# A sparse expert FFN on one core: experts dealt one by one to the shorter of two sequences, in place of two fixed lists

## What is computed

```python
logits = h @ router_w + router_b
top_v, top_i = lax.top_k(logits, 4)
top_w = softmax(top_v)
# for each expert e, over the tokens sent to it:
z = h[tok] @ w1[e] + b1[e]                 # w1[e]: 1024 x 2048
z_glu, z_lin = split(z, 2)
z_glu = min(z_glu, 7); z_lin = clip(z_lin, -7, 7)
act = z_glu * sigmoid(1.702 * z_glu) * (z_lin + 1)
y = act @ w2[e] + b2[e]                    # w2[e]: 1024 x 1024
# h + g2 * (sum of the token's four y * weight), then a final RMSNorm
```

## Time and profile before

| what | value |
|---|---|
| median of 3 runs | 1625.52 us |
| profiled execution, its own time | 1622.66 us |
| its span | 1620.8 us |
| PE busy / DVE / ACT / POOL | 91% / 45% / 16% / 13% of the span |
| weights and other data over the DMA queues | 497.13 MB, mean 307 GB/s |
| chain that ended last | PE 64%, DMA 20%, SP's queue 9%, DVE 4% |
| FFN loop, first to last step end (L1392) | 541.2 to 1583.3 us |

### The profile page before, as it was taken

The page is one execution under the profiler, slowest core; times in us unless marked ns, Lnnn a source line. Parts: engine busy times, 40 slices in busy tenths (PEclk is TensorE's granted clock), DMA queues, the critical chain, the costliest instruction groups (busy, mean ns, idle before and its releaser), DMA issues.

```text
span 1620.8 us, 39662 instructions
## 1 busy us (share of the span) xinstructions
PE 1478.6 (91%) x14640; PEld 739.7 (46%) x14640; DVE 734.9 (45%) x2468; ACT 251.7 (16%) x434; POOL 211.5 (13%) x263
## 2 busy tenths in 40 slices
PE   5999999999895988999799899999889979998897
PEld 3658888888552332333234234343233324343333
DVE  4403877777647432434244244434233424343344
ACT  4403555555322000000000000000000000000001
POOL 1000000000151111212121121212111211111120
PEclk9999999999997998999899899999799979999998
DMA  8685111112667898948989989999899989999878
GB/s 358 200 269 148 55 53 52 52 52 56 240 289 289 352 419 332 417 191 359 414 340 404 413 341 405 417 415 418 327 417 416 418 328 418 417 414 417 331 307 308
DMA packets 130869, 497.13 MB, mean 307 GB/s; under 512 B 15372, under 2 KB 48492, under 8 KB 94908
## 3 DMA queue, kind: packets, MB, share of 16 engines
q1 hardware_dynamic: 122588, 479.99, 75.2%
q0 software_dynamic: 8256, 16.81, 2.8%
HBM read 484.92 MB, written 17.58 MB: 310 GB/s over the span
## 4 chain that ended last, share of the span: by engine, by line
PE 64%; DMA 20%; SPq 9%; DVE 4%; issue 2%; ACT 1%; POOL 0%; DVEq 0%; POOLq 0%; ACTq 0%
PE ps L1777 24%; PE ps L1815 12%; DMA big_b<-in_moe_w 10%; DMA arena<-in_moe_w 8%; PE ps L1474 6%; SPq L435 6%; PE ps L1475 6%; PE ps L1476 6%; SPq L429 3%; PE ps L1653 3%; PE ps L1585 1%; PE ps L1497 1%; DMA ring_t<-in_mod_c 1%; PE ps L1599 1%; PE ps L1594 1%
## 5 line engine op out<-in xcount | busy, mean ns | idle before, releaser
L1777 PE MATMUL ps<-arena,rows 128*32 128x512 f32 x2736 | 329.7, 617 | 36.2 <-DMA arena<-in_moe_w 32.8
L1777 PE MATMUL ps<-big_b,rows 128*32 128x512 f32 x2688 | 315.8, 605 | 24.3 <-DMA big_b<-in_moe_w 23.6
L1777 PEld LDWEIGHTS ps<-arena,rows 128*32 128x32 f32 x2736 | 87.1, 112 | 231.8 <-issue 153.2
L860 ACT ACTIVATE rows<-ps 128x256 f32<-128x256 f32 x84 | 32.2, 384 | 1032.2 <-issue 636.5
L1777 PEld LDWEIGHTS ps<-big_b,rows 128*32 128x32 f32 x2688 | 85.5, 111 | 212.8 <-issue 152.7
L1815 PE MATMUL ps<-big_b,rows 128*32 128x256 f32 x2688 | 165.9, 397 | 14.9 <-DMA big_b<-in_moe_w 14.9
L1815 PE MATMUL ps<-arena,rows 128*32 128x256 f32 x2688 | 166.1, 398 | 12.5 <-DMA arena<-in_moe_w 12.5
L1392 DVE SCALAR_TENSOR_TENSOR y_sb<-ps,w_s,g_q 128x256 f32<-128x256 f32 x42 | 20.3, 484 | 288.7 <-PE ps L1815 288.7
L1392 DVE SCALAR_TENSOR_TENSOR rows<-ps,w_s,g_q 128x256 f32<-128x256 f32 x42 | 20.3, 484 | 267.7 <-PE ps L1815 267.7
L1815 PEld LDWEIGHTS ps<-big_b,rows 128*32 128x32 f32 x2688 | 84.1, 114 | 77.2 <-DMA big_b<-in_moe_w 22.8
L1815 PEld LDWEIGHTS ps<-arena,rows 128*32 128x32 f32 x2688 | 84.6, 113 | 73.6 <-DMA arena<-in_moe_w 18.9
(11 more groups left out here) (361 smaller groups left out, 1768.7 us busy)
## 6 DMA issues: line engine op xcount, KB each, us to landing
big_b<-in_moe_w SPq DMA_DIRECT2D x192, 1024.0 KB, 15.4
arena<-in_moe_w SPq DMA_DIRECT2D x192, 1024.0 KB, 16.9
ring_t<-in_hg_w_in SPq DMA_DIRECT2D x32, 512.0 KB, 4.0
ogT<-in_mod_w SPq DMA_DIRECT2D x16, 1024.0 KB, 5.1
arena<-yrows SPq DMA_DIRECT2D x8, 1024.0 KB, 12.0
x_sb<-in_x SPq DMA_DIRECT2D x2, 2048.0 KB, 7.8
arena<-in_hg_w_in SPq DMA_DIRECT2D x4, 1024.0 KB, 25.6
arena<-in_mod_c SPq DMA_DIRECT2D x4, 1024.0 KB, 22.3
```

Source lines behind the costliest of these rows:

```text
L1777: last = mm(bank[q * G:(q + 1) * G, :], XT[par][:, pos * G:(pos + 1) * G], w[:, :, q * NW:(q + 1) * NW], start=(pos == 0), stop=False)
```

## The change

Both kernels deal the 32 experts to two sides. Before, which size rank goes to which side, and where in it, is fixed by two lists (STREAM). After, there is one list of ranks (ORDER); each expert in turn goes to the side that has fewer steps so far, behind those already there. If the two sides are equal the one that was dealt to last takes the next. The running totals are a prefix scan on DVE (`so_far`) and a recursion of 32 rounds on POOL with two `tensor_scalar` each (`ahead` is the longer side's total, `minus` its negative, a wait after each round). DVE makes of it each expert's side and first pair. The gather for step one moves into the middle of POOL's recursion. The matmuls of the table (formerly ahead of `slots_of(2)`) stand behind the fourth of the six early w1 chunks (TABLE_BEHIND = 3). On DVE much of the work that followed the table stands before it now, and `tab_ok` is raised after the one-hot of step two, not before it. Step one's one-hot has a buffer of its own (`pt1`), which frees `pt` for step two. Expert 1 also has at least one group. The table is shorter (NPAIR_MAX from 94 to 56).

```diff
-NPAIR_MAX = LAT * TOPK // G + E - 2
+NPAIR_MAX = (LAT * TOPK // G + E + LAT // G) // 2
-STREAM = ((0, 2, 5, 7, 6, 18, 16, 17, 23, 15, 31, 9, 26, 28, 21, 27),
-          (1, 19, 25, 29, 11, 24, 14, 22, 20, 13, 30, 12, 10, 8, 4, 3))
+ORDER = (0, 1, 11, 13, 10, 3, 29, 15, 22, 7, 18, 6, 31, 12, 8, 21, 2,
+         19, 27, 17, 28, 9, 20, 5, 23, 16, 4, 26, 24, 14, 25, 30)
+TABLE_BEHIND = 3
...
# POOL, behind the scatters
-            for par in range(2):
-                pool.wait_ge(S["idx_ok"], par + 1)
-                gather(par)
+            pool.wait_ge(S["idx_ok"], 1)
+            gather(0)
+            pool.wait_ge(S["row_ok"], 4)
+            for j in range(E):
+                if j == E // 2:
+                    pool.wait_ge(S["idx_ok"], 2)
+                    gather(1)
+                total = so_far[:, j + 1:j + 2]
+                me.mark(pool.tensor_scalar(ahead[:, j + 1:j + 2], minus[:, j:j + 1], total, ahead[:, j:j + 1],
+                                           ALU.add, ALU.max))
+                me.mark(pool.tensor_scalar(minus[:, j + 1:j + 2], ahead[:, j:j + 1], total, minus[:, j:j + 1],
+                                           ALU.subtract, ALU.min))
+                me.wait()
+            pool.sem_inc(S["dealt_ok"], 1)
...
# DVE, behind nr16
             dve.wait_ge(S["tab_ps"], 5)
-            me.mark(V.tensor_copy(tab_nn[:, :], ps[6][0:1, 100:102]))
...
+            V.tensor_tensor_scan(so_far[:, 1:E + 1], ones[0:E, 0:E], ps[6][0:E, 96:96 + E], 0.0, ALU.mult,
+                                 ALU.add).then_inc(S["row_ok"], 1)
+            hot_tile(2, slice(1, 2), pt1)
+            hot_tile(3, slice(1, 2), pt1)
+            choice(slice(1, 2), 1)
+            dve.wait_ge(S["xi_ps"], 2)
+            index(1, False)
+            next_slots()
+            transpose_x(0, 16)
...
+            dve.wait_ge(S["dealt_ok"], 1)
+            me.mark(V.tensor_tensor(more, ahead[:, 0:E], ahead[:, 1:E + 1], ALU.not_equal))
+            me.mark(V.tensor_tensor(dealt[:, 0, :], so_far[:, 0:E], ahead[:, 0:E], ALU.subtract))
+            me.wait()
+            me.link(V.tensor_tensor_scan(behind[:, 1:E + 1], more, none[:, :], 0.0, ALU.not_equal, ALU.add))
+            me.link(V.scalar_tensor_tensor(dealt[:, 1, :], behind[:, 0:E], float(4 * E), dealt[:, 0, :], ALU.mult, ALU.add))
+            me.link(V.tensor_tensor(dealt, dealt, ident[0:E, 0:E].unsqueeze(1).broadcast_to([E, 2, E]), ALU.mult))
+            me.link(V.tensor_reduce(at_2, dealt, AX_X, ALU.add))
+            me.mark(V.tensor_scalar(stb16, at_2[:, 0:1].broadcast_to([E, P]), float(G), None, ALU.mult))
+            me.mark(V.scalar_tensor_tensor(end_c, by_rank[:, 0:1], 1.0, at_2[:, 1:2], ALU.mult, ALU.add))
+            me.link(V.tensor_scalar(past[0:E], io_c[0:E], at_2[:, 1:2], None, ALU.is_ge))
             V.scalar_tensor_tensor(ind16, io_c[0:E], end_c, past[0:E], ALU.is_lt, ALU.mult).then_inc(S["row_ok"], 1)
...
             dve.wait_ge(S["tab_ps"], 6)
             me.link(V.tensor_scalar(bef[:, :], ps[7][:, 0:NBT], float(E), None, ALU.add))
             me.mark(V.tensor_copy(tab_e[:, :], bef[0:1, :]))
+            me.mark(V.scalar_tensor_tensor(dm, ranks, 1.0, msk, ALU.add, ALU.mult))
+            me.wait()
+            dve.sem_inc(S["y_ok"], 2)
+            one_hot(2, 0)
+            choose(0, 0)
             me.mark(V.tensor_scalar(tab_ld[:, :, 0], bef[0:1, :], float(E - 1), None, ALU.min))
...
             dve.sem_inc(S["tab_ok"], 1)
...
# PE, the early chunks of step 0
             for pos in range(AHEAD):
                 z_chunk(ps[2], 0, pos, 16)
+                if pos == TABLE_BEHIND:
+                    pe.wait_ge(S["row_ok"], 5)
+                    for i in range(LT):
+                        mm(ps[3][:, i * E:(i + 1) * E], stb16, rt16, start=False, stop=True, skip_group_check=True)
+                    mm(ps[7][:, 0:NBT], idb16, ind16, start=True, stop=True).then_inc(S["tab_ps"], 1)
             slots_of(3)
```

More of the change, by code:

```diff
@@ L186, in build @@
         nmax = rtake(LT)
-        pt0 = rtake(LT * P // 2).bitcast(BF16).rearrange("p (i s) -> p i s", i=LT)
+        pt0, pt1 = (rtake(LT * P // 2).bitcast(BF16).rearrange("p (i s) -> p i s", i=LT) for _ in range(2))
         es = rtake(LT)
-        cntc, nbc, start_c = (rtake(1) for _ in range(3))
+        cntc, nbc = (rtake(1) for _ in range(2))
         thr, over = rtake(LAT // G), rtake(LAT // G)
@@ L194, in build @@
         io_one = rtake(E)[0:E]
-        pick = rtake(2 * E)[0:E].rearrange("p (a e) -> p a e", a=2)
+        so_far, ahead, minus, behind = (rtake(E + 1)[0:E] for _ in range(4))
+        more = key
+        at_2 = rtake(2)[0:E]
+        pick = dealt = rtake(2 * E)[0:E].rearrange("p (a e) -> p a e", a=2)
         by_rank = rtake(2)[0:E]
@@ L199, in half @@
             return rtake(n // 2)[0:E].bitcast(BF16)
-        nb16, idb16, stb16 = half(P), half(P), half(P)
+        nb16, idb16 = half(P), half(P)
+        stb16 = nb16
         nr16, gt16, rt16 = half(E), half(E), half(E)
@@ L218, in build @@
         tab_ld = tab_words[:, 2:2 * NBT + 2].rearrange("p (b w) -> p b w", w=2)
-        tab_nf = rtake(NBT)[0:1]
+        tab_nf = past[0:1]
         tab_nn = sb("tab_nn", [1, 2])
@@ L226, in build @@
         seq = sb("seq", [E, E])
[L227 to L230, removed]
+        rank_c = sb("rank_c", [E, 1])
+        none = sb("none", [E, E])
         pmod = sb("pmod", [P, 1])
@@ L293, in build @@
         mod_used modq_ok bias_ok yo_ps h_ok stdev2_ok f_ok hT_ps hT_a hT_d lT_ps lT_ok lg_ps shb_ok cb_ps rw_ok
-        e_v_ok e_w_ok msk_ok tab_ps row_ok tab_ok
+        e_v_ok e_w_ok msk_ok tab_ps row_ok dealt_ok tab_ok
         frow_st frow_st1 pt_ok xi_ps idx_ok rows_ok go xt_ok z_ps sig_ok at_ok y_ok
@@ L553, in _ @@
             pool.tensor_copy(mk[:, :, :, :], mkf).then_inc(S["consts"], 1)
-            for side_n, order in enumerate(STREAM):
-                for n, rank in enumerate(order):
-                    me.mark(pool.memset(seq[:, rank:rank + 1], float(side_n * 2 * E + n)))
+            for n, rank in enumerate(ORDER):
+                me.mark(pool.memset(seq[:, n:n + 1], float(rank)))
+            me.mark(pool.memset(none[:, :], 0.0))
             me.wait()
@@ L594, in _ @@
                 me.mark(pool.memset(kb_row[:, n:n + 1], float((2 - n) * FAR)))
+            for t in (so_far, ahead, minus, behind):
+                me.mark(pool.memset(t[:, 0:1], 0.0))
             me.wait()
@@ L982, in _ @@
             me.link(V.tensor_tensor(ed_t, seq[:, :], ident[0:E, 0:E], ALU.mult))
[L983 to L990, removed]
+            me.link(V.tensor_reduce(rank_c[:, :], ed_t, AX_X, ALU.add))
             me.wait()
@@ L1287, in _ @@
             me.link(V.tensor_reduce(nbc[0:E], over[0:E], AX_X, ALU.add))
-            me.link(V.tensor_tensor(nbc[0:E], nbc[0:E], ident[0:E, 0:1], ALU.max))
+            me.link(V.scalar_tensor_tensor(nbc[0:E], kb_col, 0.0, nbc[0:E], ALU.is_gt, ALU.max))
             V.tensor_copy(nb16, nbc[0:E].broadcast_to([E, P])).then_inc(S["row_ok"], 1)
@@ L1310, in _ @@
             me.mark(V.tensor_copy(idb16, by_rank[:, 1:2].broadcast_to([E, P])))
-            hot_tile(1, slice(1, 2))
+            hot_tile(1, slice(1, 2), pt1)
             dve.wait_ge(S["tab_ps"], 5)
-            me.mark(V.tensor_copy(tab_nn[:, :], ps[6][0:1, 100:102]))
[L1315 to L1321, removed]
-            choice(slice(1, 2), 1)
[L1323 to L1337, removed]
+            V.tensor_tensor_scan(so_far[:, 1:E + 1], ones[0:E, 0:E], ps[6][0:E, 96:96 + E], 0.0, ALU.mult,
+                                 ALU.add).then_inc(S["row_ok"], 1)
+            hot_tile(2, slice(1, 2), pt1)
+            hot_tile(3, slice(1, 2), pt1)
+            choice(slice(1, 2), 1)
             dve.wait_ge(S["xi_ps"], 2)
             index(1, False)
+            next_slots()
             transpose_x(0, 16)
@@ L1351, in _ @@
             me.link(V.reciprocal(es, es))
-            me.link(V.tensor_tensor(wd, wd, es.unsqueeze(2).broadcast_to([P, LT, E]), ALU.mult))
[L1353 to L1356, removed]
+            dve.wait_ge(S["dealt_ok"], 1)
+            me.mark(V.tensor_tensor(more, ahead[:, 0:E], ahead[:, 1:E + 1], ALU.not_equal))
@@ new lines, in _ @@
+            me.mark(V.tensor_copy(tab_n[:, 0:1], ahead[0:1, E:E + 1]))
+            me.mark(V.tensor_copy(kw16[:, :, 1, 0:E], wd))
+            me.wait()
+            me.link(V.tensor_tensor(wd, wd, kw16[:, :, 1, 0:E], ALU.subtract))
+            me.link(V.tensor_copy(kw16[:, :, 2, 0:E], wd))
+            me.link(V.tensor_tensor(wd, wd, kw16[:, :, 2, 0:E], ALU.subtract))
+            me.mark(V.tensor_copy(kw16[:, :, 3, 0:E], wd))
+            me.wait()
+            me.mark(V.memset(tab_nf[:, 0:2], 0.0))
@@ L1357, in _ @@
+            dve.wait_ge(S["tab_ps"], 6)
+            me.link(V.tensor_scalar(bef[:, :], ps[7][:, 0:NBT], float(E), None, ALU.add))
+            me.mark(V.tensor_copy(tab_e[:, :], bef[0:1, :]))
```

(14 more changed lines are left out.)

10 lines of the change are left out of this document (5 added, 5 removed).

## The result

The changed kernel takes **1613.34 us** (median of 5 runs, 1612.45 to 1618.39). The ratio to the kernel before is 0.9932, with a 95% interval of 0.9915 to 0.9949 (five runs of the kernel before stood beside it, median again 1625.52). The forecast was 1596.5 with a range of 1585 to 1614; the median is just inside the range, but the gain is 12.2 us where 29.0 were foretold. The profiled execution took 1612.45 us, with a span of 1610.4.

A forecast was written before the change was run, and what follows sets the result against it. TensorE (10.87 us a step) and the weight queue (30.2 us an expert) limit the loop in turns. 1622.66 - 36.5 (waits) + 6 (table) + 1.5 (tail) = 1593.7 us profiled, 1596.5 against the median; range 1585 to 1614.

The forecast's parts named there:

- What bounds the loop, and the waits: Loop: TensorE and weight queue limit it in turns; closely spaced switches cause the waits, which fall from 140.1 by 36.5 us.
- The first switch's wait: Loop, first expert switch: a wait of 2.2 us, kept in the forecast for the new order.
- PE's lower clock: Loop, close pairs: PE's clock falls to 0.79 to 0.86 behind idle time, part of the price of a pair.
- Rival 1: Loop: chained switches three steps apart overrun the queue's 0.6 us slack; at 1 us each 14 us, 1610.5; 12%.
- The table: Before the loop: the table's path runs through POOL, PE idles, and the loop starts later; +6 us, ends +3 and +15.
- floor 0.145, ceiling 0.56, taken 0.28: POOL's recursion: us per round, priced from linked writes; 32 rounds take 9.0 us (4.6 to 17.9).
- The lower clock in the first step: First loop step: PE runs at a lower clock behind its idle time, adding 1 us.
- After the recursion: Between `dealt_ok` (526.4) and PE's loop start (534.6): short DVE instructions, table matmuls, one-hot and PE's load of the pair count.
- Rival 2: Before the loop: DVE's work holds up POOL's first rounds, `dealt_ok` 4 us later, 1600.5; 10%.
- Rival 3: Before the loop: a small POOL instruction costs 1.05 us, a round 2.1, the recursion 67 us; slower, 1654.5; 5%.
- Rival 4: Dealing: a tie or size makes the deal differ from the one written; one more pair is 21.7 us, 1618; 5%.
- The tail: After the last step: final rows queue behind the last switch's weight loads; +1.5 us (0 to 5).

The follow-up runs named there:

- Run 5: Kernel before, its two fixed lists rewritten so both sides have nearly the same sequence of sizes and switch in adjacent steps; 1789.83 us, ratio 1.1013.
- runs 1: Kernel before, only its two fixed lists rewritten to the sequences the dealing gives for this input; 1591.71 us, ratio 0.9783.
- Run 6: Kernel before with lists rewritten to the dealt sequences, but side 1's last three ranks as 30, 24, 14; 1602.8 us, ratio 0.9859.
- Run 2: Changed kernel with one POOL instruction in each of the 32 rounds instead of two; 1607.54 us, ratio 0.9879.

## Why the prediction missed

- **What bounds the loop, and the waits: right.** 42 pairs and 384 loads, as 204 + 180 on the page of the changed kernel show against 192 and 192 in the earlier trace rows. Every wait of a pair was at its foretold step, 99.8 us in all against 103.6. Five more executions with this sequence of experts hold 101 to 104.3, so the forecast's 36.5 us of saving is within the spread (36 to 40). Run 5 is the harder test of the same rule. The first switch's wait is there in the kernel before and in runs 1 and 6, which have the old table (2.2 to 2.3 us), and in none of the five kernels that deal on the chip; why, no run tests. And the forecast called PE's lower clock a part of the price: PE's rows count it so, but in run 5 the queue, full all through, accounts for such a wait without it.
- **Rival 1 (gaps of 3 don't hold): wrong.** Four in a row run at 10.87 us a step. The margin was enough; its size of 0.6 us isn't shown, since the queue is busy all through (1.02).
- **The table: the step that failed.** The place was right (through POOL, DVE next, PE idle, no cover), the size wrong. The term "floor 0.145, ceiling 0.56, taken 0.28" a round measured 0.81. The price came from linked memsets, which read nothing, and the second instruction was put beside the first. Run 2 shows both faults: an instruction with column operands takes 0.36 instead of 0.09 to 0.145, and a second one adds its own 0.35. The 32 rounds took 26.4 us (the few slower ones counted) where 9.0 were put, and the gather's slot 2.0 instead of 1.3: the recursion ended at 544.4, not 526.4, which is 18.0 of the 19.0 us by which the first step's end was missed. Another 0.8 came behind the recursion. The lower clock in the first step isn't among the causes: it was put at 1 us, and from its first matmul to its end the step took 12.8 us where it took 11.8 (its first 16 matmuls 2.85 us where they took 1.92). The ceiling should have come from something that computes: the only arithmetic of POOL in the trace of before (L561 to L567, large tiles) took 1.9 to 4.1 us an instruction, and between 0.1 and those the honest range was far wider than 3 to 15 us.
- **After the recursion: right.** From `dealt_ok` (544.4) to PE's first loop matmul are 9.0 us, foretold 8.2 (526.4 to 534.6).
- **Rival 2 (POOL held up by DVE): small at most.** One POOL instruction, at 521.19, took 0.71 us instead of 0.36; it began together with a group of four DVE instructions of two inputs (521.17). The first 16 rounds took 13.5 us, the last 16, beside an idle DVE, 12.9. That is 0.6 us, not 4. The Trainium skill's rule of the shared port pair ("SBUF — State Buffer", "Who interferes with whom") is that a DVE instruction with two SBUF inputs contends with a POOL instruction that reads SBUF. The trace agrees in that one instruction and not in every one: the next, at 521.88, took 0.38 us beside the same DVE group.
- **Rival 3 (POOL's recursion is dear): the right mechanism at half its strength.** It decides from 1.3 us a round; at 0.81 it takes 17 us more than was put and leaves the kernel faster.
- **Rival 4 (another deal than written): didn't happen.** Both sides have 42 steps and every switch is in its place.
- **The tail: right place, mis-sized.** That the final rows queue behind the last weights was foretold, at 1.5 us. It's 4.9. The prediction gives no sum for its 1.5, and the rows' own time gives the size: 14.2 us, of which 4.3 lie before the last step's end, leave 9.9 behind it, where they left 5.4 before. PE's first 14 matmuls behind them then take 8.12 us instead of 7.68. That is 4.5 + 0.4 = 4.9. At the weights' 417 GB/s the 3.7 MB would have taken 9 us. Run 6 takes most of it away again (38.1 against 42.2).

## What to carry to other kernels

When loads can't run ahead, write out where they fall: a price for each spacing, read from one trace, forecast the waits of three other orders of the same work, 100 to 300 us, to within 10 us. The short sequential computation in front of this loop cost in proportion to its number of instructions (other sizes than 32x1 weren't tried), so price each instruction from one that reads operands on the same engine, and look for the form with one instruction a round (`max(total - ahead, ahead)`) before choosing the engine. And when a transfer moves behind another, take its duration from its own row, not from the best rate in the profile.
